# A two-pass mixer with sixty gathered expert rows inside it, and two alternating stages for the gate matrices

## The chip, the cores and the metric

The kernel is one launch on one core of one Trainium2 chip. The metric is device time in microseconds (us). The time given for the kernel before is the median of 3 runs, 4351.54 us (4319.0 to 4370.52).

## What is computed

One layer of a hybrid model for 1024 prompt tokens and 8 sample tokens: attention of two kinds (latent attention, and three groups of dilated windows), a gated mixer that adds their outputs to the residual, and then an expert layer. Width is 1024. What matters here is the end of the layer:

```python
y = gate_a * (o_mla @ lw['w_branch_mla']) + gate_b * (o_dil @ lw['w_branch_dil'])
x = x + gt1 * (y @ lw['w_out'])
h2 = modulate(x, lw['norm_ffn_g'], sh2, sc2)
x = x + gt2 * peer(h2, lw['w_pq'], lw['sub_keys'], lw['expert_u'], lw['expert_v'])
...
def peer(h, w_pq, sub_keys, expert_u, expert_v):
        q = (hx @ w_pq).reshape(PEER_BLOCK, PEER_HEADS, 2, PK_HALF)
        s = jnp.einsum('nhpc,hpkc->nhpk', q, sub_keys).astype(jnp.float32)
        top_s, top_i = lax.top_k(s, PEER_TOPK)
...
        best_s, best = lax.top_k(cand.reshape(PEER_BLOCK, PEER_HEADS, PEER_TOPK * PEER_TOPK), PEER_TOPK)
...
        a = jax.nn.gelu(jnp.einsum('nd,nhkd->nhk', hx, expert_u[eidx]), approximate=False) * g
        return jnp.einsum('nhk,nhkd->nd', a, expert_v[eidx])
```

The gates are sigmoids of the hidden state times `w_gate`. There are 16384 experts, and each token uses 16 experts in each of 8 heads: 128 rows of `expert_u` and 128 of `expert_v` (kept side by side in `uv`, 8 KB for a pair).

## The kernel before, in words

Tokens are cut into eight tiles of 128 and a ninth of 8. Everything of this part is kept with features on the partitions and tokens along the free side.

**The mixer, `stage_mix` (L1546).** It goes over 24 units, 8 blocks of 128 output features times 3 chunks of 344 tokens. For a unit TensorE does 8 fp32 branch products (L1630; the trace counts an fp32 matmul as two) and 48 products of split weights: a weight or activation w is kept as a rounded high part and a low part, and `product3` (L177 to L179) multiplies high by high, low by high, high by low. ScalarE makes the high part of a weight (L1579), VectorE the low part (L184); ScalarE takes the sigmoids (L1664), VectorE mixes (L1695, L1698). After all units the mixed y is split in the same way and goes through `w_out` in 24 units of 24 products. Squares, their sums over the features (L1617), roots, and the scaled h2 end the stage. All engines meet at its end.

**The expert layer, `stage_ffn` (L1832).** It has four stretches.

1. The early router: for 16 half heads (hp) the query of tiles 0 and 1 (L2356), the scores (L2346), the best 16 of 128 on VectorE (`top16`, L1954 to L1961). Then 48 transposes (L2402) turn h2 of the six sparse tiles into rows, and VectorE picks the experts of tile 0: the five pieces of `Picks`.
2. Batches. Sparse tiles (0 to 4 and the 8 sample tokens) get their experts by gathers. A batch is two gathered rows for each of 128 tokens, that is two indirect DMAs on GpSimd's queue (L2035) of 128 x 8 KB, 2.1 MB together. VectorE takes two dot products with the token's row (L2137); ScalarE applies gelu and the gate (L2219, L2222) and, for the first two tiles, writes a diagonal matrix (L2231), with which TensorE adds the rows up (L2463). Batches 3, 6, ... 45 (`ON_VEC`) are added up by VectorE instead (L2087). The ring `rows` holds five batches, and a gather waits until the sum of five batches before has read its place. Batches 0 to 47 carry the late router, one half head in three batches, for the other seven tiles (L2411, L2346, `top16`). From batch 51 on the pieces of the three dense tiles (5, 6, 7) and, from 61 on, their gate matrices are made: 96 quads (L2163, L2170, L2301, L2303, L2435), two in a batch, copied by ScalarE into `stage` (L2313) and written to DRAM (`gates_dram`) 16 quads at a time; the next block waits for that write.
3. Batch 128 on: the dense loop. Every one of 128 turns multiplies the three dense tiles with 128 experts (L2474, L2488), with 0.5 MB of `uT` and of `v` loaded for it; beside it run the remaining 196 batches, three in two turns, summed on VectorE (L2103).
4. The outputs are turned, added and stored.

The order on each engine is what this code says; the numbers of batches, pieces and quads come from the tables at L1845 to L1862.

## Time and profile before

| what | value |
| --- | --- |
| median of 3 runs | 4351.54 us |
| profiled execution | 4370.86 us, its span 4369.1 us |
| mean granted TensorE clock | 0.913 |
| PE busy | 3802.1 us (87%) |
| DVE (VectorE) busy | 2723.7 us (62%) |
| ACT (ScalarE) busy | 1199.4 us (27%) |
| moved by DMA | 1016.29 MB, 233 GB/s over the span |

PE is TensorE's matmuls, PEld its weight loads, POOL GpSimd, SP the queue that issues most loads. A busy share over the whole span says little here, since the stretches have different limits; they have to be read one by one.

### The profile page before, as it was taken

How to read it: one execution, taken by the hardware profiler on the slowest of the kernel's cores; microseconds unless marked ns; L12 is line 12 of the kernel's file. 1: busy time of each engine (PE TensorE's matmuls, PEld its weight loads, DVE VectorE, ACT ScalarE, POOL GpSimd, SP SyncE). 2: the span in 40 equal slices, each digit the busy share in tenths (PEclk: the TensorE clock that was granted, in tenths of full speed). 3: DMA queues.
4: the chain of work that ended last, by engine and by line, in shares of the span. 5: the costliest groups of instructions: out<-in, count | busy, mean ns of one | idle time of the engine just before them, and what ended most of it. 6: DMA issues, size and time to landing. Idle time of an engine off the chain costs nothing.

```text
span 4369.1 us, 43255 instructions
## 1 busy us (share of the span) xinstructions
PE 3802.1 (87%) x14474; PEld 2490.1 (57%) x14474; DVE 2723.7 (62%) x6374; ACT 1199.4 (27%) x3244; POOL 859.8 (20%) x718
## 2 busy tenths in 40 slices
PE   8798899999981899967997677799999999899896
PEld 7575377888970788953453444344454444445443
DVE  2764562533534111258999987767779676967876
ACT  2564432322332111122222567421111111111111
POOL 0000000001000000003333223333333333344332
PEclk8898998995985899988999888899999999999997
DMA  4001102203116111237888879999999999999997
GB/s 158 7 1 42 29 37 80 81 20 119 51 40 208 55 41 36 100 108 282 323 327 318 314 302 376 399 417 409 410 399 378 414 412 387 384 409 412 387 354 279
DMA packets 255851, 1016.29 MB, mean 233 GB/s; under 512 B 28650, under 2 KB 103810, under 8 KB 170642
## 3 DMA queue, kind: packets, MB, share of 16 engines
q0 software_dynamic: 101520, 723.10, 41.9%
q1 hardware_dynamic: 131218, 280.65, 17.4%
q10 hardware_dynamic: 22896, 9.80, 0.8%
q8 instruction: 117, 1.92, 0.2%
q14 instruction: 100, 0.82, 0.1%
HBM read 964.22 MB, written 49.25 MB: 232 GB/s over the span
## 4 chain that ended last, share of the span: by engine, by line
PE 27%; DVE 15%; DMA 11%; issue 2%; ACT 2%; SPq 0%; POOL 0%; ACTq 0%; DVEq 0%
PE banks L2488 9%; PE banks L2474 9%; DMA ff_room<-in_v 7%; PE banks L2463 4%; DVE ff_rows L2137 4%; PE banks L2411 2%; DVE ff_acc L2103 2%; DMA gates_dram<-ff_room 2%; PE banks L2356 1%; DMA ff_rows<-in_uv,pk_expert 1%; DVE pk_eq L1793 1%; DVE pk_axes L1798 1%; DVE mx_x L2163 1%; PE banks L2435 1%; DVE pk_besti L1772 1%
## 5 line engine op out<-in xcount | busy, mean ns | idle before, releaser
L2035 POOL DMA_INDIRECT ff_rows<-in_uv,pk_expert x640 | 803.0, 1255 | 1519.2 <-DVE ff_acc L2103 831.8
L2137 DVE CUSTOM_DVE_ANT_0 ff_rows<-ff_rows,ff_h_row 128x1024 f32<-128x1024 f32 x648 | 766.6, 1220 | 45.3 <-DMA ff_rows<-in_uv,pk_expert 43.4
L2488 PE MATMUL banks<-ff_room,mx_x 128*128 128x512 f32 x1536 | 702.3, 608 | 57.9 <-DVE mx_x L2178 31.2
L2474 PE MATMUL banks<-mx_x,ff_room 128*128 128x384 f32 x2048 | 685.7, 488 | 12.2 <-ACT mx_x L2321 12.2
L2463 PE MATMUL banks<-ff_rows,o_mla_tops 128*128 128x512 f32 x904 | 446.5, 643 | 144.5 <-ACT o_mla_tops L2231 140.8
L2474 PEld LDWEIGHTS banks<-mx_x,ff_room 128*128 128x128 f32 x2048 | 390.3, 191 | 313.0 <-issue 77.3
L2488 PEld LDWEIGHTS banks<-ff_room,mx_x 128*128 128x128 f32 x1536 | 297.3, 195 | 418.9 <-issue 357.8
L2103 DVE SCALAR_TENSOR_TENSOR ff_acc<-ff_rows,ff_a,ff_acc 128x1024 f32<-128x1024 f32 x388 | 498.6, 1285 | 7.2
L2463 PEld LDWEIGHTS banks<-ff_rows,o_mla_tops 128*128 128x128 f32 x904 | 179.1, 206 | 361.8 <-issue 198.5
L177 PE MATMUL banks<-d_w_high,h_high 128*128 128x512 f32 (+1 forms) x648 | 274.3, 423 | 21.9 <-DVE d_w_low L184 21.0
L2219 ACT ACTIVATE ff_gelu<-ff_dots 128x2 f32<-128x2 f32 x324 | 65.7, 203 | 824.9 <-DVE ff_dots L2137 824.7
L178 PE MATMUL banks<-d_w_low,h_high 128*128 128x512 f32 (+1 forms) x648 | 264.4, 408 | 0.0
L179 PE MATMUL banks<-d_w_high,h_low 128*128 128x512 f32 (+1 forms) x648 | 263.8, 407 | 0.0
L2178 DVE TENSOR_TENSOR mx_x<-mx_x 128x384 f32<-128x384 f32 x128 | 71.3, 557 | 293.8 <-DMA mx_x<-gates_dram 162.1
L2321 ACT ACTIVATE mx_x<-banks 128x384 f32<-128x384 f32 x128 | 62.6, 489 | 626.0 <-PE banks L2474 626.0
L754 DVE TENSOR_TENSOR banks<-banks,masks 128x128 f32<-128x128 f32 (+1 forms) x160 | 53.6, 335 | 255.0 <-PE banks L665 240.3
L177 PEld LDWEIGHTS banks<-d_w_high,h_high 128*128 128x128 f32 (+1 forms) x648 | 166.5, 257 | 46.6 <-DVE d_w_low L184 10.4
L179 PEld LDWEIGHTS banks<-d_w_high,h_low 128*128 128x128 f32 (+1 forms) x648 | 166.7, 257 | 20.4
L178 PEld LDWEIGHTS banks<-d_w_low,h_high 128*128 128x128 f32 (+1 forms) x648 | 167.7, 259 | 18.2
L2411 PE MATMUL banks<-mx_x,ff_room 128*128 128x388 f32 x512 | 173.3, 491 | 0.0
L1695 DVE TENSOR_TENSOR mx_t<-mx_sig,banks 128x344 f32<-128x344 f32 x48 | 22.4, 509 | 236.6 <-ACT mx_sig L1664 236.6
L2222 ACT ACTIVATE ff_a<-ff_gelu,pk_gate 128x1 f32<-128x1 f32 x640 | 153.5, 287 | 11.0
(391 smaller groups left out, 5660.3 us busy)
## 6 DMA issues: line engine op xcount, KB each, us to landing
ff_room<-in_uT SPq DMA_DIRECT2D x128, 512.0 KB, 14.4
ff_room<-in_v SPq DMA_DIRECT2D x128, 512.0 KB, 20.6
gates_dram<-ff_room SPq DMA_DIRECT2D x6, 4096.0 KB, 16.8
mx_x<-gates_dram SPq DMA_DIRECT2D x128, 192.0 KB, 17.2
d_w<-in_w_dil POOLq DMA_DIRECT2D x9, 2048.0 KB, 8.3
d_w<-in_w_ada POOLq DMA_DIRECT2D x32, 512.0 KB, 4.7
ff_room<-in_w_pq SPq DMA_DIRECT2D x32, 512.0 KB, 4.5
ff_rows<-in_uv,pk_expert POOLq DMA_INDIRECT x640, 10.8
```

Source lines behind the costliest of these rows:

```text
L177: pe.matmul(out, w[0], x[0], start=start, stop=False)
L178: pe.matmul(out, w[0], x[1], start=False, stop=False)
L179: return pe.matmul(out, w[1], x[0], start=False, stop=stop)
L2035: pool.indirect_dma_start(out=rows[r][:, :], out_offset=None, in_=IN["uv"][:, :], in_offset=bass.IndirectOffsetOnAxis(ap=at, axis=0))\
L2103: ins = dve.scalar_tensor_tensor(out=y[:], in0=v, scalar=weight, in1=y[:], op0=ALU.mult, op1=ALU.add)
L2137: ins = dve.tensor_tensor_reduce(rows[r][:, 0:D], rows[r][:, 0:D], h_row[i % 2][:], 1.0, 0.0, ALU.mult, ALU.add, dots[:, B % RB, j:j + 1])
L2178: dve.tensor_tensor(blocks(ad[e % 2]), blocks(ge[e % 2]), g2[e // 2 % 2][:, :, :, e % 2], ALU.mult)\
L2222: ins = act.activation(a[:, B % RB, j:j + 1], act_of[:, B % RB, j:j + 1], ACT.Copy, scale=gt[:, b * G + j:b * G + j + 1])
L2411: ins = pe.matmul(Q[:, i, 0:CL], w[n % 2][:, k, :], c.h2[:, k, NE + i * CL:NE + (i + 1) * CL], start=(k == 0), stop=(k == KD - 1))
L2463: ins = pe.matmul(A[:, half], diag[:, n % DB, j], rows[r][:, D + half * 512:D + (half + 1) * 512], **ends)
L2474: ins = pe.matmul(SD[:, 0:ND], u[e % 4][:, k, :], hd[:, k, :], start=(k == 0), stop=(k == KD - 1))
L2488: ins = pe.matmul(Y[j][:, half], ad[e % 2][:, j * P:(j + 1) * P], v[e % 4][:, half_rows[half]], start=(e == 0), stop=(e == NK - 1))
```

## The change

`stage_mix` is written anew. Pass 0 takes tiles 0 and 1 (256 tokens, `NE`) through the gates, through `w_out`, to h2. Pass 1 takes the other 776 tokens in two chunks of 388. A unit is now one side (one of the two branches) of one block of features and one chunk: 16 in pass 0, 32 in pass 1. Each weight is loaded and split in both passes. After the second unit of pass 1 the whole early router stands on TensorE, ScalarE and VectorE (here with the names `mx_rows` for its space and `px_` for its picks), then 8 transposes for the rows of tile 0, and on VectorE the pieces of tile 0. From unit z = 5 of pass 1 on, 30 batches (60 gathered rows for each token of tile 0) run in the mixer: 24 beside gate units, 6 beside output units. Their dots and sums are both VectorE's. Their ring holds two batches.

```diff
 PAGE, NPAGE, PAST = 128, 8, 1024
 PH, NK, TOPK = 8, 128, 16
...
     nc, IN = c.nc, c.IN
-    KO = GW // P
+    KO, HP, G, NE = GW // P, 2 * PH, 2, EARLY * P
+    CB = (TOK - NE) // 2
+    PASSES = [[(0, NE)], [(NE, NE + CB), (NE + CB, TOK)]]
+    SUBS = [(p, m, side, i) for p in range(2) for m in range(KD) for side in range(2) for i in range(len(PASSES[p]))]
+    OUTS2 = [(p, m, i) for p in range(2) for m in range(KD) for i in range(len(PASSES[p]))]
+    S1, O1, W1 = 2 * KD, KD, 3 * KD
+    NB, RB = MIX_BATCHES, 2
+    ROUTER_AT = 1
+    BATCH_AT = [z for z in range(5, 31) if z not in (16, 28)] + list(range(33, 48, 2))
+    batch_at = {z: b for b, z in enumerate(BATCH_AT[0:NB])}
...
+        ringR, ring = same_place(c, ctx, [P, RB * G, 2 * D], [("mx_rows_high", F32R), ("mx_rows", F32)])
...
+                    if m == 2:
+                        sp.dma_start(keys, IN["keysT"]).then_inc(s["keys_in"], 16)
+                    if m == 3:
+                        queries(0)
...
+                for n in range(S1, S1 + 4):
+                    weight(n)
+                sp.wait_ge(s["mm"], S1)
+                residual(0)
+                for n in range(S1 + 4, W1):
+                    weight(n)
+                branch(KD)
+                branch(KD + 1)
+                weight(W1)
+                weight(W1 + 1)
+                keep(0)
+                weight(W1 + 2)
+                for n in range(2, HP):
+                    queries(n)
+                weight(W1 + 3)
+                for m in range(2, KD):
+                    branch(KD + m)
...
+            @block.gpsimd
+            def _(pool):
+                pool.wait_ge(s["half_tile"], 1)
+                for b in range(NB):
+                    for j in range(G):
+                        r = b % RB * G + j
+                        if b >= RB:
+                            pool.wait_ge(s["rsum"], (b - RB) * G + j + 1)
+                        at = c.expert0[:, b * G + j:b * G + j + 1]
+                        pool.indirect_dma_start(out=ring[:, r, :], out_offset=None, in_=IN["uv"][:, :],
+                                                in_offset=bass.IndirectOffsetOnAxis(ap=at, axis=0))\
+                            .then_inc(rows_in[r], 16)
...
+                def gated(u):
+                    p, m, side, i = SUBS[u]
+                    c0, c1 = PASSES[p][i]
+                    n, b = p * W1 + 2 * m + side, p * KD + m
+                    gate, out = c.ps[2 * (u % 3)][:, 0:c1 - c0], c.ps[2 * (u % 3) + 1][:, 0:c1 - c0]
...
+                    if S1 <= u < S1 + 3:
+                        pe.wait_ge(s["out"], (O1 - 2, O1, O1)[u - S1])
...
+                    if u >= 3:
+                        pe.wait_ge(s["y"], u - 2)
+                    src = c.o_dilT if side else c.o_mlaT
+                    for k in range(KO):
+                        pe.matmul(out, wb[b % 2][:, side * KO + k, :], src[:, k, c0:c1], start=(k == 0), stop=(k == KO - 1))
+                    pe.wait_ge(s["w_lo"], n + 1)
+                    for k in range(KD):
+                        ins = product3(pe, gate, w_parts(n, k), [t[:, k, c0:c1] for t in h_parts], k == 0, k == KD - 1)
+                    ins.then_inc(s["mm"], 1)
...
+                for u in range(S1):
+                    gated(u)
+                pe.wait_ge(s["y"], S1)
+                for v in range(O1):
+                    projected(v)
+                squares_sum(0, KD - 1)
+                for u in range(S1, len(SUBS)):
+                    gated(u)
+                    if u == S1 + ROUTER_AT:
+                        pe.wait_ge(s["keys_in"], 16)
+                        pe.wait_ge(s["h2"], KD)
+                        queries(0)
+                        for hp in range(HP):
+                            if hp + 1 < HP:
+                                queries(hp + 1)
+                            scores(hp)
...
+                def weights(b):
+                    act.wait_ge(s["dot"], b + 1)
+                    act.activation(act_of[:, b % RB], dots[:, b % RB], ACT.Gelu).then_inc(s["gelu"], 1)
+                    act.wait_ge(s["gelu"], b + 1)
+                    for j in range(G):
+                        ins = act.activation(a[:, b % RB, j:j + 1], act_of[:, b % RB, j:j + 1], ACT.Copy,
+                                             scale=c.gate0[:, b * G + j:b * G + j + 1])
+                    ins.then_inc(s["a"], 1)
...
+                for z in range(len(SUBS) - S1):
+                    sigmoid(S1 + z)
+                    for n in made_after(S1 + z):
+                        w_high(act, n)
+                    if z == ROUTER_AT:
+                        copied_queries(0)
...
+                    if z == 3:
+                        pk.exps(act, 0)
+                    if z in batch_at:
+                        weights(batch_at[z])
...
+                def dot(b):
...
+                    if b >= RB:
+                        dve.wait_ge(s["a"], b - RB + 1)
+                    for j in range(G):
+                        r = b % RB * G + j
+                        dve.wait_ge(rows_in[r], 16 * (b // RB + 1))
+                        u = ring[:, r, 0:D].rearrange("p (k n) -> p k n", n=NE)
+                        ins = dve.tensor_tensor_reduce(u, u, h_row, 1.0, 0.0, ALU.mult, ALU.add, dots[:, b % RB, j:j + 1])
+                    ins.then_inc(s["dot"], 1)
...
+                def sums(b):
+                    dve.wait_ge(s["a"], b + 1)
...
+                        else:
+                            dve.wait_ge(s["rsum"], b * G + j)
+                            ins = dve.scalar_tensor_tensor(out=acc, in0=v, scalar=weight, in1=acc, op0=ALU.mult, op1=ALU.add)
+                        ins.then_inc(s["rsum"], 1)
+
+                def sums_due(z):
+                    if z in batch_at and batch_at[z]:
+                        sums(batch_at[z] - 1)
+
+                def dots_due(z):
+                    if z in batch_at:
+                        dot(batch_at[z])
...
+                for z in range(len(SUBS) - S1):
+                    sums_due(z)
+                    mixed(S1 + z)
+                    for n in made_after(S1 + z):
+                        w_low(dve, n)
+                    if z == ROUTER_AT:
+                        for hp in range(HP):
+                            dve.wait_ge(s["sc_copy"], hp + 1)
+                            for part in range(4):
+                                top16(part, hp)
+                                dve.wait_ge(s["top"], hp * 4 + part + 1)
+                        pk.prepare(dve)
+                        picks(0)
+                        picks(1)
+                    if 2 <= z <= 4:
+                        picks(z)
+                    dots_due(z)
+                y_low(1)
+                w_low(dve, W1 + 2 * KD + 1)
+                for m in range(KD):
+                    for n in made_beside(1, m):
+                        if n > W1 + 2 * KD + 1:
+                            w_low(dve, n)
+                    for i in range(2):
+                        sums_due(32 + 2 * m + i)
+                        added(O1 + 2 * m + i)
+                        dots_due(32 + 2 * m + i)
+                sums(NB - 1)
+                normed(1)
```

In `stage_ffn` tile 0 keeps batches 30 to 63 only, so that tile 1 begins at batch 34 (by the new numbering, which is used for the changed kernel from here on) and the dense loop at 98. Three quads are made in a batch, from batch 58 to 89. The gate blocks go to two stages in turn; the second lies in four of the ten gather rows, and from batch 56 to 95 the ring therefore holds three batches (`FEW`). VectorE's own sums (`ON_VEC`) stand at batches 3 to 30. The rows of tiles 2 to 4 and of the samples are stored by SP, not by GpSimd.

```diff
-    batches = [(i, b) for i in range(NS) for b in range(TAILB if i == TAIL else PER)]
-    first = [batches.index((i, 0)) for i in range(NS)] + [len(batches)]
-    ORDER = [0, 1] + DENSE + [2, 3, 4, NT - 1]
+    batches = [(i, b) for i in range(NS) for b in range(0 if i else MIX_BATCHES, TAILB if i == TAIL else PER)]
+    first = [batches.index((i, 0 if i else MIX_BATCHES)) for i in range(NS)] + [len(batches)]
+    ORDER = [1] + DENSE + [2, 3, 4, NT - 1]
...
-    PICK0, HOT0, HOTS = HP * LATE_PER + 3, HP * LATE_PER + 13, 2
+    PICK0, HOT0, HOTS = HP * LATE_PER + 3, HP * LATE_PER + 10, 3
...
-    TURN0 = 112
+    TURN0 = 86
     OUT_AT = 44
-    PIECES = {4 + 8 * k: (1, k) for k in range(5)}
-    PIECES |= {PICK0 + 10 * j + 2 * k: (t, k) for j, t in enumerate(DENSE) for k in range(5)}
-    PIECES |= {PICK0 + 59 + 3 * k: (2, k) for k in range(5)}
+    PIECES = {2 + 6 * k: (1, k) for k in range(5)}
+    PIECES |= {PICK0 + at + step * k: (t, k) for t, at, step in zip(DENSE, (0, 6, 16), (1, 2, 2)) for k in range(5)}
+    PIECES |= {PICK0 + 29 + 3 * k: (2, k) for k in range(5)}
     PIECES |= {first[i + 1] - 12 + 2 * k: (SPARSE[i + 1], k) for i in range(ON_PE, TAIL - 1) for k in range(5)}
...
-    ON_VEC = list(range(LATE_PER, HP * LATE_PER, LATE_PER))
+    ROWS_ORDER = [0] + list(range(2, NS)) + [1]
+    ON_VEC = list(range(LATE_PER, first[1] - 1, LATE_PER))
...
+    FEW, FEW_AT, MANY_AT = 3, HOT0 - 2, HOT0 + QUADS // HOTS + 6
+    place = [B % FEW if FEW_AT <= B < MANY_AT else (B - (0 if B < FEW_AT else first[TAIL])) % RB for B in range(len(batches))]
...
-        stage = part(0, NK * GBLK).rearrange("p (a n) -> p a n", n=GBLK)
+        second = ring[:, FEW * G:FEW * G + 4].rearrange("p r f -> p (r f)")
+        stage = [t.rearrange("p (a n) -> p a n", n=GBLK) for t in (part(0, NK * GBLK), second)]
...
                     sp.wait_ge(s["hot_copy"], (k + 1) * BQ)
-                    sp.dma_start(gates[k].rearrange("p a n -> p (a n)"), stage.rearrange("p a n -> p (a n)"))\
-                      .then_inc(s["g_out"], 16)
-                sp.wait_ge(s["g_out"], 16 * (QUADS // BQ))
+                    sp.dma_start(gates[k].rearrange("p a n -> p (a n)"), stage[k % 2].rearrange("p a n -> p (a n)"))\
+                      .then_inc(g_out[k % 2], 16)
+                for k in range(2):
+                    sp.wait_ge(g_out[k], 16 * (QUADS // BQ // 2))
...
-                    if B - RB in ON_VEC:
-                        pool.wait_ge(s["early"], by_vec(B - RB) * G)
-                    elif RB <= B < BP + RB:
-                        pool.wait_ge(s["psum"], by_pe(B - RB))
-                    elif B >= RB:
-                        pool.wait_ge(s["sum"], (B - RB - BP + 1) * G)
-                    if B == PER // 2:
-                        pool.wait_ge(pk.done, 1)
+                    if B == MANY_AT:
+                        pool.wait_ge(g_out[1], 16 * (QUADS // BQ // 2))
+                    if last[B] in ON_VEC:
+                        pool.wait_ge(s["early"], by_vec(last[B]) * G)
+                    elif last[B] is not None and last[B] < BP:
+                        pool.wait_ge(s["psum"], by_pe(last[B]))
+                    elif last[B] is not None:
+                        pool.wait_ge(s["sum"], (last[B] - BP + 1) * G)
...
+                                act.wait_ge(s["top"], 4 * HP)
+                            elif q == BQ:
+                                act.wait_ge(s["psum"], by_pe(FEW_AT - 1))
                             else:
-                                act.wait_ge(s["g_out"], 16 * (q // BQ))
+                                act.wait_ge(g_out[q // BQ % 2], 16 * (q // BQ // 2))
```

Three places show what the engines now have in a row. The first is TensorE where the mixer ends and the expert layer begins. Before, with the router's queries (L2356) ahead of the transposes (L2402):

```order
4517 L1617 MATMUL banks<-o_mla_tops,ones 128x344 x6
4518 L1589 UNCONDITIONAL_BRANCH
4519 L2336 UNCONDITIONAL_BRANCH
4520 L2356 MATMUL banks<-mx_x,ff_room 128x256 x16
4521 L2346 MATMUL banks<-ff_room 128x128 x2
...
4547 L2346 MATMUL banks<-ff_room 128x128 x2
4548 L2356 MATMUL banks<-mx_x,ff_room 128x256 x8
4549 L2346 MATMUL banks<-ff_room 128x128 x4
4550 L2402 MATMUL banks<-ident,mx_x 128x128 x24
4551 L2402 MATMUL banks<-ident,mx_x 8x128 x8
4552 L2402 MATMUL banks<-ident,mx_x 128x128 x16
4553 L2411 MATMUL banks<-mx_x,ff_room 128x388 x6
4554 L2463 MATMUL banks<-ff_rows,o_mla_tops 128x512 x4
```

and in the changed kernel (L2707 is a transpose, L2719 a late query, L2771 a sum of gathered rows):

```order
4554 L182 MATMUL banks<-mx_y_high,mx_w_low 128x388
4555 L1729 MATMUL banks<-o_mla_tops,ones 128x388 x4
4556 L1641 UNCONDITIONAL_BRANCH
4557 L2658 UNCONDITIONAL_BRANCH
4558 L2707 MATMUL banks<-ident,mx_x 128x128 x32
4559 L2707 MATMUL banks<-ident,mx_x 8x128 x8
4560 L2707 MATMUL banks<-ident,mx_x 128x128 x8
4561 L2719 MATMUL banks<-mx_x,ff_room 128x388 x6
4562 L2771 MATMUL banks<-ff_rows,o_mla_tops 128x512 x4
```

The queries and scores of 16 half heads have left this place; the 48 transposes stand first.

The second is VectorE in pass 1 of the mixer, where before only weights were split (L184) and units mixed (L1695, L1698):

```order
1587 L1695 TENSOR_TENSOR mx_t<-mx_sig,banks 128x344 x2
1588 L1698 TENSOR_TENSOR mx_y<-mx_t 128x344
1589 L184 TENSOR_TENSOR mx_w_low<-mx_w,mx_w_high 128x2048
1590 L1695 TENSOR_TENSOR mx_t<-mx_sig,banks 128x344 x2
1591 L1698 TENSOR_TENSOR mx_y<-mx_t 128x344
1592 L1695 TENSOR_TENSOR mx_t<-mx_sig,banks 128x344 x2
1593 L1698 TENSOR_TENSOR mx_y<-mx_t 128x344
```

In the changed kernel, from the unit z = 7 on (L1996 a dot, L2007 a sum of a gathered row into tile 0's total, which lies in `region`, L1927 to L1930 the mixing, L187 the low part of a weight):

```order
1823 L2007 SCALAR_TENSOR_TENSOR region<-mx_rows,mx_a,region 128x1024 x2
1824 L1929 TENSOR_TENSOR mx_sig<-mx_sig,banks 128x388
1825 L1930 TENSOR_TENSOR mx_y<-mx_y,mx_sig 128x388
1826 L1996 ISA mx_rows,mx_dots<-mx_rows,o_mla_tops 128x1024
1827 L1996 ISA mx_dots 128x1
1828 L1996 ISA mx_rows,mx_dots<-mx_rows,o_mla_tops 128x1024
1829 L1996 ISA mx_dots 128x1
1830 L2007 SCALAR_TENSOR_TENSOR region<-mx_rows,mx_a,region 128x1024 x2
1831 L1927 TENSOR_TENSOR mx_y<-mx_sig,banks 128x388
1832 L187 TENSOR_TENSOR mx_w_low<-mx_w,mx_w_high 128x1024
1833 L1996 ISA mx_rows,mx_dots<-mx_rows,o_mla_tops 128x1024
1834 L1996 ISA mx_dots 128x1
```

Between two units there now stand two dots and two sums.

The third is ScalarE beside it, again of the changed kernel (L1823 the sigmoid, L1622 the high part of a weight, L1864 gelu, L1867 the gate):

```order
1038 L1823 ACTIVATE mx_sig<-banks 128x388
1039 L1864 ACT_TABLE_LOAD
1040 L1864 ACTIVATE mx_gelu<-mx_dots 128x2
1041 L1867 ACTIVATE mx_a<-mx_gelu,region 128x1 x2
1042 L1823 ACT_TABLE_LOAD
1043 L1823 ACTIVATE mx_sig<-banks 128x388
1044 L1622 ACTIVATE mx_w_high<-mx_w 128x1024
1045 L1864 ACT_TABLE_LOAD
1046 L1864 ACTIVATE mx_gelu<-mx_dots 128x2
1047 L1867 ACTIVATE mx_a<-mx_gelu,region 128x1 x2
1048 L1823 ACT_TABLE_LOAD
```

A table load stands before each sigmoid and before each gelu; before, the mixer's gate units had one in all.

## Rows read from the trace of the kernel before

**Rows 1.** Windows by stage; columns: length, then busy us (instructions) of each engine, clock, DMA
```profile
core 0: us, PE busy (x) PEld busy (x) DVE busy (x) ACT busy (x) POOL busy (x), PEclk, DMA share, GB/s
1448.60:1877.80 429.20, 403.69 (x2160) 356.44 (x2160) 103.39 (x149) 70.93 (x93) 0.00 (x0) 0.97 0.15 54
1877.80:1976.80 99.00, 79.94 (x367) 65.31 (x368) 59.31 (x300) 18.70 (x43) 2.15 (x4) 0.86 0.37 123
1976.80:2334.40 357.60, 314.73 (x980) 169.46 (x979) 326.93 (x1206) 86.58 (x287) 111.98 (x104) 0.96 0.84 319
2334.40:2892.70 558.30, 417.87 (x1451) 230.10 (x1450) 468.98 (x1328) 297.22 (x768) 180.49 (x162) 0.87 0.89 351
2893.00:4321.00 1428.00, 1354.09 (x3608) 690.08 (x3607) 1084.75 (x1577) 197.33 (x714) 524.30 (x393) 0.98 1.00 397
```
**Rows 2.** Timeline of PE: split products of 344 columns in the mixer, of 512 earlier
```profile
1602.04 0.32 PE L179 MATMUL banks<-h_high,mx_w_low 128*128 128x344 f32 x1
...
1609.10 0.32 PE L179 MATMUL banks<-h_high,mx_w_low 128*128 128x344 f32 x1
...
699.88 0.39 PE L177 MATMUL banks<-d_w_high,h_high 128*128 128x512 f32 x1
...
702.66 0.39 PE L177 MATMUL banks<-d_w_high,h_high 128*128 128x512 f32 x1
```
**Rows 3.** Chain of waits, early router: start, us, what (one half head of sixteen)
```profile
1893.74 3.71 PE banks L2356 x16
1898.06 3.71 PE banks L2356 x16
```
**Rows 4.** Chain of waits, late router: one half head, three batches
```profile
2218.88 7.82 PE banks L2411 x24
2226.70 3.43 PE banks L2463 x8
...
2235.69 3.63 PE banks L2463 x8
2239.32 7.82 PE banks L2411 x24
```
**Rows 5.** Timeline of DVE: picks of tile 0, and dots and sums in the dense loop
```profile
1961.02 1.23 DVE L1765 TENSOR_TENSOR pk_cand<-o_mla_tops 128x1024 f32<-128x1024 f32 x1
1977.36 0.23 DVE L1815 SCALAR_TENSOR_TENSOR pk_expert<-pk_axes 128x64 uint32<-128x64 f32 x1
1995.71 0.22 DVE L1815 SCALAR_TENSOR_TENSOR pk_expert<-pk_axes 128x64 uint32<-128x64 f32 x1
...
2951.24 1.22 DVE L2137 CUSTOM_DVE_ANT_0 ff_rows<-ff_rows,ff_h_row 128x1024 f32<-128x1024 f32 x1
2952.39 2.64 DVE L2103 SCALAR_TENSOR_TENSOR ff_acc<-ff_rows,ff_a,ff_acc 128x1024 f32<-128x1024 f32 x2
2960.08 0.56 DVE L2178 TENSOR_TENSOR mx_x<-mx_x 128x384 f32<-128x384 f32 x1 [2.75 <-DMA mx_x<-gates_dram]
```
**Rows 6.** Timeline of ACT: a table load, gelu and gate of the first batch
```profile
1994.81 1.28 ACT L2219 ACT_TABLE_LOAD   x1
1998.38 0.20 ACT L2219 ACTIVATE ff_gelu<-ff_dots 128x2 f32<-128x2 f32 x1 [2.29 <-DVE ff_dots L2137]
1998.62 0.48 ACT L2222 ACTIVATE ff_a<-ff_gelu,pk_gate 128x1 f32<-128x1 f32 x2
```
**Rows 7.** Windows from batch 51 to the dense loop; then VectorE's waits there, longest first
```profile
2352.20:2892.70 540.50, 403.18 (x1409) 223.29 (x1408) 453.57 (x1261) 290.06 (x743) 173.39 (x155) 0.87 0.89 353
...
DVE ff_rows L2137 <- DMA ff_rows<-in_uv,pk_expert: 43.4, 24, 5.3
DVE mx_x L2163 <- PE banks L2435: 35.0, 6, 9.8
```
**Rows 8.** DMA issues in the mixer and in the late router: size, median us to landing
```profile
mx_w<-in_w_gate SPq DMA_DIRECT2D x12, 512.0 KB, 5.5
...
ff_rows<-in_uv,pk_expert POOLq DMA_INDIRECT x88, 8.1
```

635 lines of the change are left out of this document (386 added, 249 removed).

## The prediction

> **What bounds the kernel now.** I read the windows by stage first [rows 1], since the shares over the whole span mix stretches with different limits. The mixer takes 429.2 us, and TensorE is busy in 403.7 of them: it is the bound, VectorE is busy for a quarter, and the DMA engines for 0.15. The early router and the turning of rows take 99.0 us, again nearly all TensorE's. Then come 357.6 us of batches under the late router. There the chain of waits steps by 20.44 us for one half head and three batches (2218.88 to 2239.32), and all but 1 us of a step is on TensorE [rows 4]. The next 558.3 us belong to VectorE, busy for 469.0. The dense loop has a DMA share of 1.00 at 397 GB/s: TensorE is busy for 1354 of 1428 us beside it, but the bytes set the pace [rows 1].
>
> So the kernel has a mixer in which the DMA engines idle and a dense loop in which they are full. The change takes 30 of the 64 batches of tile 0 out of the stretch before the dense loop and puts them beside the mixer. The dense loop keeps its 196 batches, its 128 turns and its bytes: I take its 1428 us, and everything before the mixer, as unchanged.
>
> **The mixer.** TensorE's work first. A split product of 344 columns comes every 0.157 us (45 of them in 7.06 us), one of 512 every 0.232 (12 in 2.78) [rows 2]. The trace has none of 256 or 388 columns; on the line through the two they are 0.118 and 0.177. Bounds for the 256 ones: 0.116 if they went with the columns alone (0.232 x 256 / 512), and 0.157 if something other than the columns sets the pace below 344, which no row excludes; the 192 + 384 products of pass 0 would then cost 22 us more. I take the line, since 344 and 512 lie close to one rate. A half of an fp32 product costs 7.82 / 24 = 0.326 us at 388 columns [rows 4], so 0.289 at 344, and 3.71 / 16 = 0.232 at 256 [rows 3].
>
> - Before: 24 units of 48 x 0.157 + 16 x 0.289 = 12.2, 292 us; 24 output units of 24 x 0.157 and 48 halves for the squares, 104. Together 396; the other 33 us are the start, the splitting of y between the two parts, and the end (roots, reciprocals, h2).
> - After: pass 0 has 16 units of 24 x 0.118 + 8 x 0.232 = 4.7, 75 us, and 8 output units of 3.3, 26. Pass 1 has 32 units of 24 x 0.177 + 8 x 0.326 = 6.85, 219 us, and outputs of 16 x 4.24 + 32 x 0.326 = 78. Together 398: cutting the tokens in two costs TensorE 2 us. The ends, now with two changes from gates to outputs but fewer columns in the last, are 34. Weights are loaded and split twice. A weight lands in 5.5 us [rows 8] and pass 0 has four places for them, so this hides behind units of 4.7 us; if it did not, each of 16 weights would cost up to 1 us.
> - The root, the reciprocal and h2 of pass 0 (about 10 us) hide behind the first two units of pass 1, 13.7 us. Then the router: 16 x 4.32 us [rows 3], and with its filling and 8 transposes 73 us. It stays pure TensorE time, as before.
> - After it VectorE is late. It ends the last `top16` about 3.7 us after TensorE's scores, and the first half of the picks is 16.5 us (1961.02 to 1977.6 [rows 5]); then it mixes and splits the weight of the third pair, at 22. TensorE needs that weight after its transposes, two units and four branch products, at 18.3. The second half of the picks is 18.4 us (1977.4 to 1995.9) and delays the next weight likewise, by 7. I charge 11 us.
> - From then on a unit with a batch costs VectorE two dots of 1.15 and the read (2.38), the wait for gelu and gate (0.72 on ScalarE [rows 6], 0.85 with signals), two sums 2.6, mixing 0.56 or twice that (0.87 in the mean), half a low part 0.6 (it has the 1024 columns of a dot), and 0.15 for signals: 7.45 us [rows 5]. TensorE needs 6.85. Over the 27 units from z = 5 on this is 24 x 7.45 + 3 x 1.5 = 183 against 185, with three banks' worth of slack between the engines. Balanced, then; I charge 10 us for what two balanced engines lose to each other here and beside the outputs. The added wait is the one for the gate, at the head of the sums: behind it on VectorE stand the mixing and the low part, for which TensorE waits.
> - The gathers: from the end of the first sum of a batch to the first dot two batches on VectorE has 10.2 us of other work; a landing takes 8.1 [rows 8]. Hidden, by a small margin.
> - ScalarE now has two table loads of 1.28 us [rows 6] a unit. With gelu and gate 0.7, sigmoid 0.5, half a high part 0.5, that is 4.3 of 7.45, and the load for gelu has no dependency and runs ahead of its wait, as the one at 1994.81 did. Cost: nothing.
>
> The Trainium skill ("ScalarE: Activation LUTs", What ACT_TABLE_LOAD costs) speaks against this: a switch costs 2.66 us, since a drain of 1.38 us goes with the load. By that ScalarE would need 7.1 us a unit, and the mixing would wait 0.3 us a unit for its sigmoid, 7 us in all. The row shows 1.28 and no drain, but the engine was idle behind it, so the trace doesn't decide.
>
> Sum: 398 + 73 + 11 + 10 + 34 = 526 us for 429.2, so **+97**.
>
> **The expert layer up to the dense loop.** Before, batch 51 begins 474.4 us after the stage's start (2352.2 less 1877.8). After: the 48 transposes are 22 us (99.0 less 69 for the half heads, less some 8 for the first weights and the filling [rows 1, 3]), and 3 go to a store in their middle. These stores now stand in SP's queue ahead of the third query weight, which is wanted 40 us later. The gathers start with the stage, so TensorE doesn't wait for the first batch as it did. 11 half heads of 20.44 and, because `ON_VEC` ends with batch 30, 5 that carry a third batch on TensorE, each 3.43 more [rows 4]: 344 us. Then 18 us of `top16` and dots as before (2334.4 to 2352.2). 387: **-87**, of which 70 is the router that moved into the mixer.
>
> From batch 51 on VectorE was busy for 453.6 of 540.5 us [rows 7]. Quads and pieces stay as many; 30 batches go, 60 dots of 1.15 = 69 us, leaving 385. Of its 87 us of idle time 35.0 were waits for quads behind a gate block that was being written, 43.4 waits for gathered rows [rows 7]. The second stage removes the 35, since a block now has five batches until its place is wanted again. The waits for rows I leave at 40: fewer batches, but a shorter ring. 385 + 40 + 8 = 433: **-107**.
>
> Total: 97 - 87 - 107 = -97 us on the profiled 4371, 4274. That run was slow against the median 4351.54; the same 2.2% of it gives **4255 us**.
>
> **The rivals.**
>
> 1. The rings are too short. From batch 56 to 95 a gather waits for the sum three batches before: dots 2.3, gelu, gate and diagonal 1.4, sum 3.43, two issues 2.5, landing 8.1 make 17.7 us, and ScalarE can be late with the quads by 5. Three batches of 9.2 (433 / 47) are 27.6, but batches without a piece are near 7, and a gate block of 4 MB in front can double a landing. For: VectorE waited 24 times for rows even with five batches. Price: 3 us in 20 batches, 60 us; and in the mixer a landing of 14 instead of 8.1 costs (14 - 10.2) / 2 in 30 batches, 57. One of them gives 4313, both 4371.
> 2. The other way, the rings keep up, the waits for rows fall with the load (40 to 10), and TensorE and VectorE lose nothing to each other: 4274 - 40, scaled 4215 or less.
> 3. Slower than before: the ring of two in the mixer decides alone. It cancels the gain where a landing takes 10.2 + 2 x 97 / 30 = 16.7 us, and passes 1% at 19.6 (44 us more, 4395). The mixer also reloads 17 MB, but its DMA share is 0.15 and the gathers add about 0.7; a median of 8.1 at a share of 0.84 [rows 1, 8] speaks against it.
> 4. The table switches cost the page's price: 4262.
>
> **Chances.** The sum as made (4215 to 4300) 0.55, too-short rings 0.20, better 0.15, slower 0.05, table switches 0.05. A measurement of this kernel can tell about 1% from no change. Faster by over 1% (below 4308) takes the first, the third, the last and a quarter of the rings: 0.80; within 1% 0.15; slower 0.05. The range, 4190 to 4335, leaves out the worse half of the rings and the slower case.
>
> **What would show it.** In the changed profile: the mixer ends near 1975 us; split products of 256 columns come every 0.118 us; gate units of pass 1 with a batch come every 7 to 7.6 us, TensorE stands still twice after the router, 4 and 7 us; the first dense product is near 2795, with the dense loop still at 1428 us; ScalarE's waits for the gate write are gone; VectorE's waits for rows before the dense loop are near 40 us, and few in the mixer. Wrong would be: units of 9 us or more, waits for rows over 80 us, or a dense loop whose length moved by more than 20 us, since its bytes did not.

## The result, and the profile of the changed kernel

| what | before | after |
| --- | --- | --- |
| median | 4363.84 us (4319.0 to 4371.42, 11 runs) | 4293.51 us (4259.48 to 4309.49, 11 runs) |
| ratio to before | 1 | 0.985, 95% interval 0.9821 to 0.9879 |
| span of the profiled execution | 4369.1 us | 4302.4 us |

The changed kernel is faster by 1.5%, where the prediction said 2.2% (4255 of 4351.54; range 4190 to 4335). Both profiles have the same mean clock, 0.913, so their stages can be set side by side: 66.7 us less in the span, for 97 forecast. Part of the distance between 4255 and 4293.51 is not the kernel's: the forecast was scaled to 4351.54, the median of 3 runs of before, and over 11 runs that median is 4363.84.

The windows by stage of the changed kernel answer to [rows 1]: the mixer with the early router in it; the transposes; the rest of the late router; batch 51 to the first dense product; the dense loop with the outputs (length, busy us of PE, PEld, DVE, ACT, POOL, clock, DMA share, GB/s).

```profile
core 0: us, PE busy (x) PEld busy (x) DVE busy (x) ACT busy (x) POOL busy (x), PEclk, DMA share, GB/s
1448.60:1973.30 524.70, 475.40 (x2482) 415.99 (x2480) 354.26 (x727) 203.73 (x327) 100.85 (x60) 0.96 0.60 216
1973.30:2003.70 30.40, 12.71 (x47) 7.81 (x48) 8.68 (x14) 6.55 (x11) 9.37 (x10) 0.50 0.97 384
2003.70:2373.60 369.90, 346.50 (x1068) 183.95 (x1066) 304.18 (x1201) 96.38 (x321) 109.30 (x101) 0.99 0.81 304
2373.60:2825.10 451.50, 316.81 (x1166) 190.55 (x1165) 382.24 (x1141) 249.17 (x592) 101.91 (x94) 0.83 0.73 281
2825.10:4302.40 1477.30, 1365.12 (x3657) 697.63 (x3655) 1114.10 (x1636) 203.63 (x729) 528.21 (x394) 0.97 0.98 388
```

| stretch, us | before | forecast | after |
| --- | --- | --- | --- |
| mixer, up to the turning of rows (before: up to the stage's end) | 429.2 | 526 | 524.7 |
| expert layer's start to batch 51 | 474.4 | 387 | 400.3 |
| batch 51 to the first dense product | 540.5 | 433 | 451.5 |
| from there to the end | 1475.5 | same | 1477.3 |

The mixer's row is cut at 1448.60 us, where the mixer of before begins. In the changed kernel the first branch product stands at 1445.5, so its own mixer takes 527.9 us and the code ahead of it, which is not changed, 3.1 us less; it spreads by far more than that (see the experiments). From the first branch product to the end it is 2920.5 us before and 2856.9 after, 63.6 less.

So the mixer came out within 2 us of its forecast by either cut, and the loop did not move. The missing 30 us lie in the two stretches between.

**The mixer.** TensorE's timeline in pass 0 (start, us, line, shapes) shows a split product of 256 columns, of which [rows 2] had none:

```profile
1499.96 0.28 PE L181 MATMUL banks<-h_low,mx_rows_high 128*128 128x256 f32 x1
...
1500.89 0.28 PE L180 MATMUL banks<-h_high,mx_rows_high 128*128 128x256 f32 x1
```

Eight products in 0.93 us: one every 0.116 (0.1175 over five others), for 0.118 forecast. In pass 1 a unit with 388 columns begins here and the next one there:

```profile
1745.94 0.64 PE L180 MATMUL banks<-h_high,mx_w_high 128*128 128x388 f32 x1
...
1750.32 0.34 PE L182 MATMUL banks<-h_high,mx_w_low 128*128 128x388 f32 x1
1750.50 2.77 PE L1747 MATMUL banks<-o_dilT,mx_w_branch 128*128 128x388 f32 x8
1752.80 0.64 PE L180 MATMUL banks<-h_high,mx_w_high 128*128 128x388 f32 x1
```

A unit takes 6.86 us, TensorE's own 6.85 of the forecast, and not VectorE's 7.45. Two windows, one behind the router and one over the units with batches:

```profile
1645.00:1690.00 45.00, 35.39 (x147) 28.36 (x148) 41.13 (x117) 9.00 (x12) 4.35 (x4) 0.89 0.35 129
1690.00:1867.00 177.00, 176.72 (x820) 148.89 (x819) 146.59 (x191) 99.19 (x153) 78.58 (x46) 0.99 0.86 312
```

In the first TensorE stands still for 9.6 us (2.87 and 6.75, for 4 and 7 forecast) and waits for the low part of a weight, since VectorE picks experts. In the second it is busy for 176.72 of 177 us beside 2.1 MB of gathered rows a unit, at a DMA share of 0.86. The ring of two, in which the slower case lay, is never waited for at length: of VectorE's waits in the whole mixer this line is all of that kind.

```profile
DVE mx_rows L1996 <- DMA mx_rows<-in_uv,region: 5.9, 7, 2.3
```

**Between the mixer and the dense loop.** The chain of waits at the stage's start (start, us, what) shows the turning of rows (L2707) with two long stores in it.

```profile
1984.17 11.30 DMA h_rows<-ff_h_row
...
1997.80 4.56 DMA h_rows<-ff_h_row
...
2003.04 1.11 PE banks L2707 x4
```

ScalarE can overwrite its place for turned rows (L2585) only when SP's store of them has landed. The window from 1973.30 to 2003.70 above has a DMA share of 0.97: the gathers of five batches, 10.5 MB, start at the same time (experiment 7 holds four of them back).

Behind the transposes ScalarE's copy of a query (L2520) marks each half head: the first at 2023.47 us, the sixteenth at 2356.35. Of the fifteen steps between them six are the forecast's 20.44 to 0.01 us and the last four its 23.87, with three sums in each:

```profile
2311.45 3.63 PE banks L2771 x8
2315.08 3.91 PE banks L2719 x12
...
2329.77 2.62 PE banks L2719 x8
...
2335.33 3.63 PE banks L2771 x8
```

But one step is 26.50 us, from 2105.41 to 2131.91. In it the chain lies on VectorE, with picks of tile 1 (L2096 to L2110), dots, sums and the late `top16` in a row:

```profile
2107.00 1.24 DVE pk_cand L2096
...
2114.50 1.61 DVE pk_besti L2110 x4
...
2122.29 1.21 DVE region L2411
```

The step of 21.60 has picks in its chain too (L2119 to L2135). The one of 25.59 lies on TensorE: a third sum, and 1.72 us of four products (L2766) that take over VectorE's sums of tile 0 where its batches end. With these two the fifteen take 332.9 us where the forecast's are 324 (ten of 20.44 and five of 23.87).

VectorE's waits from batch 51 to the dense loop answer to [rows 7] (us, times, longest):

```profile
DVE ff_rows L2460 <- DMA ff_rows<-in_uv,pk_expert: 60.1, 16, 15.5
DVE ff_rows L2460 <- DMA ff_rows<-in_uv,region: 2.5, 2, 1.4
DVE mx_x L2486 <- PE banks L2743: 1.2, 1, 1.2
```

The 35.0 us behind the gate blocks are 1.2, as said. Its busy time is 382.24 us, for 385. But the waits for rows are 62.6, for 40. The timeline shows where they lie: 12 us in one place, at batches 58 and 59,

```profile
2431.07 1.23 DVE L2460 CUSTOM_DVE_ANT_0 ff_rows<-ff_rows,ff_h_row 128x1024 f32<-128x1024 f32 x1 [9.68 <-DMA ff_rows<-in_uv,pk_expert]
...
2434.68 1.23 DVE L2460 CUSTOM_DVE_ANT_0 ff_rows<-ff_rows,ff_h_row 128x1024 f32<-128x1024 f32 x1 [2.38 <-DMA ff_rows<-in_uv,pk_expert]
```

9 us at two gate blocks (2532 and 2637 us), and 42 us in the last 57 before the dense loop. That last part has a bound of its own, in the changed kernel and before the change:

```profile
2768.50:2825.10 56.60, 32.02 (x60) 12.74 (x59) 14.82 (x25) 9.87 (x36) 19.71 (x18) 0.85 0.95 381
```

```profile
2836.00:2893.60 57.60, 44.30 (x89) 18.46 (x90) 37.40 (x65) 18.02 (x58) 22.43 (x20) 0.85 1.02 419
```

The first line is the changed kernel's, the second that of before. VectorE, which bounds the stretch as a whole, has 15 us of work in 57 (before: 37 in 58), at a DMA share of 0.95 (1.02).

### The profile page after: what moved, and what is told of

Read it like the earlier page. It is cut to its first block, busy times and chain, and to the rows that moved or that the text cites. A ratio compares the mean times of both kernels' runs of the same rounds, so it can differ in the third digit from the quotient of the medians.

```text
span 4302.4 us, 43216 instructions
## 1 busy us (share of the span) xinstructions
PE 3735.0 (87%) x14282; PEld 2465.9 (57%) x14282; DVE 2813.1 (65%) x6473; ACT 1282.9 (30%) x3304; POOL 888.3 (21%) x714
## 4 chain that ended last, share of the span: by engine, by line
PE 23%; DVE 15%; DMA 13%; issue 2%; ACT 1%; SPq 0%; POOL 0%; DVEq 0%; ACTq 0%; POOLq 0%
DMA ff_room<-in_v 9%; PE banks L2796 8%; PE banks L2782 8%; DVE ff_rows L2460 4%; PE banks L2771 3%; PE banks L2719 3%; DVE mx_x L2486 2%; DMA ff_rows<-in_uv,pk_expert 2%; DMA mx_x<-gates_dram 1%; DVE region L2426 1%; DVE pk_eq L2124 1%; DVE o_mla_tops L2129 1%; DVE mx_x L2493 1%; DVE ff_acc L2426 1%; DVE pk_besti L2110 1%
## 5 line engine op out<-in xcount | busy, mean ns | idle before, releaser
L2460 DVE CUSTOM_DVE_ANT_0 ff_rows<-ff_rows,ff_h_row 128x1024 f32<-128x1024 f32 x588 | 696.5, 1221 | 86.9 <-DMA ff_rows<-in_uv,pk_expert 61.0
L2371 POOL DMA_INDIRECT ff_rows<-in_uv,region x324 | 418.6, 1292 | 808.6 <-DVE region L2426 540.9
L2371 POOL DMA_INDIRECT ff_rows<-in_uv,pk_expert x256 | 314.2, 1227 | 754.0 <-PE banks L2771 414.6
L2771 PE MATMUL banks<-ff_rows,o_mla_tops 128*128 128x512 f32 x704 | 356.7, 655 | 95.1 <-ACT o_mla_tops L2554 95.1
L2426 DVE SCALAR_TENSOR_TENSOR region<-ff_rows,ff_a,region 128x1024 f32<-128x1024 f32 x254 | 326.5, 1286 | 4.7
L2542 ACT ACTIVATE ff_gelu<-ff_dots 128x2 f32<-128x2 f32 x294 | 59.5, 203 | 846.0 <-DVE ff_dots L2460 845.8
L2771 PEld LDWEIGHTS banks<-ff_rows,o_mla_tops 128*128 128x128 f32 x704 | 142.2, 210 | 270.7 <-issue 152.6
L757 DVE TENSOR_TENSOR banks<-banks,region 128x128 f32<-128x128 f32 (+1 forms) x160 | 53.6, 335 | 256.8 <-PE banks L668 240.0
L1719 POOL DMA_INDIRECT mx_rows<-in_uv,region x60 | 100.8, 1681 | 508.7 <-DVE region L2146 342.9
L2719 PE MATMUL banks<-mx_x,ff_room 128*128 128x388 f32 x512 | 175.1, 493 | 0.0
## 6 DMA issues: line engine op xcount, KB each, us to landing
gates_dram<-ff_rows SPq DMA_DIRECT2D x3, 4096.0 KB, 15.9
```

Source lines behind the costliest of these rows:

```text
L1719: pool.indirect_dma_start(out=ring[:, r, :], out_offset=None, in_=IN["uv"][:, :], in_offset=bass.IndirectOffsetOnAxis(ap=at, axis=0))\
L2371: pool.indirect_dma_start(out=rows[r][:, :], out_offset=None, in_=IN["uv"][:, :], in_offset=bass.IndirectOffsetOnAxis(ap=at, axis=0))\
L2426: ins = dve.scalar_tensor_tensor(out=y[:], in0=v, scalar=weight, in1=y[:], op0=ALU.mult, op1=ALU.add)
L2460: ins = dve.tensor_tensor_reduce(rows[r][:, 0:D], rows[r][:, 0:D], h_row[i % 2][:], 1.0, 0.0, ALU.mult, ALU.add, dots[:, place[B], j:j + 1])
L2719: ins = pe.matmul(Q[:, i, 0:CL], w[n % 2][:, k, :], c.h2[:, k, NE + i * CL:NE + (i + 1) * CL], start=(k == 0), stop=(k == KD - 1))
L2771: ins = pe.matmul(A[:, half], diag[:, n % DB, j], rows[r][:, D + half * 512:D + (half + 1) * 512], **ends)
```

## Experiments

All times are set beside the changed kernel, 4293.51 us. Every profile is split like the table above, each at its own instructions. What lies ahead of the mixer is the same code in all of them, and takes from 1403.5 us (granted clock 0.88 there) to 1452.8 us (0.85). That is 49 us, over 1% of a kernel's time, without any edit; so differences are read from stretches and not from the whole. The last column leaves that part out. It is one profile of each kernel.

| kernel | median, us | ratio to before | first branch product to the end, us |
| --- | --- | --- | --- |
| changed | 4293.51 | 0.985 | 2856.9 |
| 1 one stage | 4308.0 | 0.9877 | 2866.3 |
| 2 blocks in four parts | 4287.08 | 0.9851 | 2854.8 |
| 2 blocks not written | 4283.54 | 0.9821 | 2831.1 |
| 3 exponentials later | 4299.6 | 0.985 | 2858.2 |
| 4 ends of the ring | 4288.66 | 0.9815 | 2849.8 |
| 5 twelve batches | 4361.73 | 0.9991 | 2909.3 |
| 6 sums on VectorE | 4276.21 | 0.9796 | 2833.6 |
| 7 gathers held | 4297.11 | 0.9851 | 2852.4 |
| 8 no table switches | 4292.02 | 0.9863 | 2848.3 |

Of the intervals given below only that of experiment 5 is clear of the changed kernel's (0.9821 to 0.9879). For all the others a difference in the kernel's whole time is not shown.

### 1. One stage, a ring of five

```diff
-    FEW, FEW_AT, MANY_AT = 3, HOT0 - 2, HOT0 + QUADS // HOTS + 6
+    FEW, FEW_AT, MANY_AT = 5, HOT0 - 2, HOT0 + QUADS // HOTS + 6
...
-        stage = [t.rearrange("p (a n) -> p a n", n=GBLK) for t in (part(0, NK * GBLK), second)]
+        stage = [t.rearrange("p (a n) -> p a n", n=GBLK) for t in (part(0, NK * GBLK),)] * 2
...
-                                act.wait_ge(g_out[q // BQ % 2], 16 * (q // BQ // 2))
+                                act.wait_ge(g_out[(q // BQ - 1) % 2], 16 * ((q // BQ + 1) // 2))
```

> Undoes the second stage alone: one stage for the gate blocks, the ring keeps five batches, three quads in a batch as in the changed kernel. Theory A (a 4 MB gate write in front of the gathers makes them land late, and three batches are too few to cover it): VectorE's waits for rows from batch 51 to the dense loop fall from 62 us to 10 to 25, but waits for quads behind the write return, 50 to 70 us, so the stretch is 450 to 470 us for 451, the kernel 0 to 20 us slower than the changed one. Theory B (the second stage is worth the 35 us of the sum): 30 us slower or more, stretch over 480.

Measured 4308.0 us, ratio to before 0.9877 (0.983 to 0.9923). VectorE's waits from batch 51 on:

```profile
DVE mx_x L2483 <- PE banks L2738: 42.6, 11, 8.6
DVE ff_rows L2457 <- DMA ff_rows<-in_uv,pk_expert: 22.1, 6, 11.9
DVE ff_rows L2457 <- DMA ff_rows<-in_uv,region: 3.0, 2, 1.6
```

The waits for quads are back, 42.6 us, but those for rows fall from 62.6 to 25.1, and the stretch is 455.7 us for 451.5. So the second stage removes what it was to remove and gives nearly all of it back through the four gather rows that it takes: it is worth 4 us in this stretch. The waits for rows that are left all lie behind 2798 us, in the last 35 us before the dense loop.

### 2. Gate blocks written in four parts, and not at all

```diff
-                    sp.dma_start(gates[k].rearrange("p a n -> p (a n)"), stage[k % 2].rearrange("p a n -> p (a n)"))\
-                      .then_inc(g_out[k % 2], 16)
+                    for j in range(4):
+                        if j:
+                            sp.wait_ge(s["dot"], HOT0 + (16 * k + 15) // HOTS + 2 + j)
+                        rows_of = slice(j * NK // 4, (j + 1) * NK // 4)
+                        sp.dma_start(gates[k][:, rows_of], stage[k % 2][:, rows_of]).then_inc(g_out[k % 2], 16)
```

> The changed kernel with each gate block written in four DMAs of 1 MB instead of one of 4 MB, the second to fourth waiting for the dots of the next three batches. Theory A (a gather stands behind 4 MB of gate block): waits for rows in that stretch fall from 62 us to 20 to 35, stretch 451 to about 420, kernel 25 to 35 us faster than the changed one. Rival (the ring of three is too short by itself, with any traffic): waits stay over 50 us, no change within 10 us.

Measured 4287.08 us, ratio 0.9851 (0.9798 to 0.9905): the stretch is 448.0 us, the waits for rows 58.9, those at the two blocks 5.3 us for 8.9. That a gather stands behind 4 MB in one piece is not what makes most of the 62.6 us. The other kernel writes a 128th of each block and takes the gates from elsewhere, so it leaves the gate matrices out of the result:

```diff
-                    sp.dma_start(gates[k].rearrange("p a n -> p (a n)"), stage[k % 2].rearrange("p a n -> p (a n)"))\
-                      .then_inc(g_out[k % 2], 16)
+                    sp.dma_start(gates[k][:, 0], stage[k % 2][:, 0]).then_inc(g_out[k % 2], 16)
...
-                            src = gates[half * GB:(half + 1) * GB, :, e:e + 2].rearrange("b p a n -> p b a n")
+                            src = IN["xT"][:, half * GB:(half + 1) * GB, 0:2 * GBLK].rearrange("p b (a n) -> p b a n", n=GBLK)
```

> The changed kernel with the gate blocks not written (32 KB of each remain) and the dense loop loading other values of the same size and row length in their place: it leaves the gate matrices out of the result. Ring, quads and copies stay as they are. Theory A (gathers land late behind the block writes): waits for rows from batch 51 on fall from 62 us to under 15, the stretch from 451 to about 400 us. Rival (the short ring by itself): waits stay over 45 us, stretch over 435.

Measured 4283.54 us, ratio 0.9821 (0.9768 to 0.9874). Its waits:

```profile
DVE ff_rows L2459 <- DMA ff_rows<-in_uv,pk_expert: 45.9, 12, 11.6
DVE ff_rows L2459 <- DMA ff_rows<-in_uv,region: 2.5, 2, 1.4
```

Without any write 48 of 62.6 us are still there; the stretch is 438.3 us, 13 less. The 12 us at batches 58 and 59 are unchanged (9.45 and 2.42 us), those at the two blocks are gone, and the last ones fall from 42 to 37. That is the rival on record (waits over 45 us, a stretch over 435), though the stretch is 13 us shorter.

### 3. Exponentials a batch later

In the changed kernel the chain went through ScalarE at these blocks: it stood for a piece's exponentials (L2141), then made three quads, and only then took gelu of the next batch (L2542), so that the sum that frees the ring came late.

```profile
2504.45 0.31 ACT pk_best L2141
...
2508.42 2.73 ACT ff_room L2635 x3
2511.16 1.28 ACT L2542
...
2519.17 15.93 DMA ff_rows<-in_uv,pk_expert
```

```diff
-                    if B in PIECES and PIECES[B][1] == 3:
-                        pk.exps(act, PIECES[B][0])
+                    if B - 1 in PIECES and PIECES[B - 1][1] == 3:
+                        pk.exps(act, PIECES[B - 1][0])
```

> The changed kernel, but ScalarE takes the exponentials of a piece one batch later, behind the next batch's gelu, gate and diagonal instead of ahead of them. Theory (the ring of three is short because ScalarE stands waiting for a piece's differences, makes three quads, and only then the gate of the next batch, so that TensorE's sum and with it the gather come late): VectorE's waits for rows between batch 51 and the dense loop fall from 62.6 to 25 to 35 us, that stretch from 451.5 to 420 to 430, the kernel is 20 to 30 us shorter than the changed one. Rival (the ring and the landings alone are too slow for a batch of 9 us, whatever ScalarE does): waits for rows stay at 55 or more, the time within 6 us.

Measured 4299.6 us, ratio 0.985 (0.9819 to 0.9882): the rival. The stretch is 450.7 us and the waits for rows are 58.9. Of the 3.7 us less, 3.2 are at batches 58 and 59 (8.9 for 12.1), and only 0.3 at the two blocks (8.5 for 8.9). The chain at the same block now has no ScalarE work of that kind, but a longer landing:

```profile
2506.73 3.71 PE banks L2771 x8
2510.71 1.09 POOL ff_rows L2371
2512.10 17.45 DMA ff_rows<-in_uv,pk_expert
2529.57 1.23 DVE ff_rows L2460
```

The gather starts 1.0 us behind the block, whose write was issued at 2511.13, where in the changed kernel it started 2.5 us behind it (2519.17 and 2516.72). It takes 17.45 us to land instead of 15.93. So in both kernels it lands 18.4 us behind the block's issue (at 2529.55 and 2535.10). In these 18.4 us 7.1 MB are moved, at a DMA share of 0.97 (here 7.2 MB in 18.5 us, share 0.96): the block's 4.2 MB and 2.9 MB of rows. The bytes decide when it lands, and ScalarE's place in the chain, which looked like the cause, was worth 0.3 us of waits at the blocks. VectorE now waits 3.1 us for the exponentials themselves.

### 4. The two ends of the ring of three

With the places of the ring written out, batch 57 takes place 0 of the ring of three, the place of batch 55, two before it; 58 is queued behind it on GpSimd. At the other end batches 96 and 97 take the places of 94 and 95, and wait for the last block's write as well.

```diff
-    FEW, FEW_AT, MANY_AT = 3, HOT0 - 2, HOT0 + QUADS // HOTS + 6
-    place = [B % FEW if FEW_AT <= B < MANY_AT else (B - (0 if B < FEW_AT else first[TAIL])) % RB for B in range(len(batches))]
+    FEW, FEW_AT, MANY_AT = 3, HOT0, first[2] + 3
+    place = [(B - FEW_AT) % FEW if FEW_AT <= B < MANY_AT else (B - (0 if B < FEW_AT else first[TAIL])) % RB for B in range(len(batches))]
```

> The changed kernel with the two changes of the ring placed otherwise: the ring of three begins at batch 58 instead of 56, its places counted so that every batch takes the place of the one three before (in the changed kernel batch 57 takes the place of 55, two before, and 58 stands queued behind it), and it ends at batch 101 instead of 96 (there batches 96 and 97 take the places of 94 and 95, two before, and wait for the write of the last gate block as well). Theory (the waits for rows come not from the ring of three as such, but from its two ends: 12 us at batches 58 and 59, and a gather that stands 21 us before batch 96): VectorE's waits for rows between batch 51 and the dense loop fall from 62.6 to 30 to 40 us, the first 12 us vanish, that stretch from 451.5 to 425 to 435, the kernel is 15 to 25 us shorter than the changed one. Rival (the end is limited by bytes: the last gate block of 4 MB, seven batches and the first loads of the dense loop): only the first 12 us go, waits near 50, stretch near 440. Second rival (what is saved is waited for again in the dense loop's first turns): the stretch shrinks and the rest grows by as much.

Measured 4288.66 us, ratio 0.9815 (0.9786 to 0.9844), 5 us less than the changed kernel where the theory said 15 to 25. The stretch is 437.8 us, 13.7 less, with waits of

```profile
DVE ff_rows L2460 <- DMA ff_rows<-in_uv,pk_expert: 44.8, 15, 15.5
DVE ff_rows L2460 <- DMA ff_rows<-in_uv,region: 4.8, 2, 2.7
```

The 12 us are gone (0.6 left). The ones before the dense loop are not (39 us for 42): the first rival, and its forecast of 440. The second rival has a part in it too: within the dense loop VectorE waits 9.2 us for rows, where the changed kernel had 0.9, and the rest takes 1480.1 us for 1477.3. The windows of this kernel, up to the last block and from there to the first dense product, say why:

```profile
2378.50:2765.00 386.50, 281.50 (x1111) 178.51 (x1110) 367.40 (x1118) 241.15 (x564) 83.07 (x77) 0.84 0.71 274
2765.00:2816.30 51.30, 30.68 (x56) 12.00 (x56) 14.25 (x23) 7.85 (x29) 14.43 (x14) 0.80 1.01 408
```

In the last 51 us the DMA share is 1.01, at 408 GB/s, and VectorE has 14 us of work. The quads and pieces are done, and what is left is bytes: a gate block, the rows of the last batches and the first loads of the dense loop, 20.9 MB (51.3 x 408). A gathered batch of 2.1 MB costs 5.1 us at that rate, where its two dots cost 2.3.

The bytes are not the whole of it. In both kernels GpSimd starts no gather for 12.73 us just ahead of this window (up to 2764.62 here, to 2770.23 in the changed kernel). It waits for TensorE's sums, which stand behind a piece, the last quads and their copies on VectorE and ScalarE. From 2762 to 2769 us the changed kernel has a DMA share of 0.37. Then the block, three batches and the first loads start together, and the longest wait of all, 15.5 us, follows. No run takes this pause away, so how much of the 39 us it makes is not shown.

### 5. Twelve batches in the mixer instead of thirty

```diff
-EARLY, MIX_BATCHES = 2, 30
+EARLY, MIX_BATCHES = 2, 12
```

> The changed kernel with 12 batches in the mixer instead of 30 (18 more in the expert layer, five more half heads with a batch summed by VectorE). My account (TensorE bounds the mixer and the batches hide behind it): mixer 525 to 510 to 517 us; the expert layer up to the dense loop 18 batches of about 8 to 9 us longer, less 17 for the half heads, +130; kernel 115 to 130 us slower than the changed one. Rival (the gathers cost the mixer what they save later): mixer shorter by 60 us or more, kernel slower by under 70.

Measured 4361.73 us, ratio 0.9991 (0.9964 to 1.0017): with twelve batches nothing is left of the gain. Its windows, the mixer, the stretch from batch 51, and the end of that stretch:

```profile
1438.00:1957.20 519.20, 475.84 (x2489) 418.71 (x2490) 268.76 (x620) 160.35 (x248) 38.57 (x24) 0.97 0.43 147
2339.70:2879.40 539.70, 383.81 (x1315) 216.55 (x1314) 426.57 (x1214) 274.96 (x683) 144.06 (x131) 0.87 0.77 304
2800.00:2879.40 79.40, 60.25 (x128) 23.66 (x129) 39.03 (x64) 20.64 (x75) 37.04 (x31) 0.98 1.01 421
```

The mixer is 9 us shorter than the changed kernel's (527.9, from its first branch product), 0.5 us a batch: they are hidden there. (The same mixer code takes 524.8 to 532.2 us in eleven profiles, so it is 0.3 to 0.7.) The stretch from batch 51 is 88 us longer, 44 of it VectorE's work and 44 waits for rows (106.2 for 62.6 us), and the late router ahead of it 16 shorter; the dense loop with the outputs is 9 shorter too. From the mixer's start to the end 52 us, by medians 68: a batch that is moved is worth 2.9 to 3.8 us.

The forecast of 115 to 130 us was too high by about two. It priced a batch in this stretch at 8 to 9 us, the mean of batches that have quads and pieces beside them. Those stay; a batch more costs 4.9 us (88 / 18). That is near the price of its bytes: in the last 79 us the DMA share is 1.01 at 421 GB/s, which makes 5.0 us for 2.1 MB, and VectorE works for 39. And since twelve batches in the mixer only bring the time of before, the rest of the rewriting, two passes and a router in the mixer, brings nothing by itself. By the slope of 2.9 to 3.8 us a batch it would cost 35 to 45 us, an estimate: no kernel without any batch in the mixer was run.

### 6. Every third batch of tile 1 on VectorE

```diff
-    ON_VEC = list(range(LATE_PER, first[1] - 1, LATE_PER))
+    ON_VEC = list(range(LATE_PER, first[1] - 1, LATE_PER)) + list(range(first[1] + 2, HP * LATE_PER, LATE_PER))
+    VEC1 = len([n for n in ON_VEC if n < first[1]])
...
-                        if B + 1 == first[1]:
-                            pe.wait_ge(s["early"], len(ON_VEC) * G)
+                        if B + 1 in (first[1], first[2]):
+                            pe.wait_ge(s["early"], (VEC1, len(ON_VEC))[i] * G)
```

> The changed kernel with batches 36, 39, 42 and 45, of tile 1, summed on VectorE too, so that half heads 12 to 15 have two batches on TensorE instead of three. My step (TensorE bounds these half heads, 3.43 us each for the third batch): four steps of 23.87 us become 20.44, the late router 352 to about 338 us, the kernel 10 to 14 us faster. Rival (VectorE is the bound there as well): no change, under 4 us.

Measured 4276.21 us, ratio 0.9796 (0.9732 to 0.986). The late router behind the transposes takes 355.4 us for 369.9, and the chain has the step of 20.44 again (2298.15 to 2318.59):

```profile
2298.15 7.82 PE banks L2726 x24
...
2318.59 7.82 PE banks L2726 x24
```

That is 14.5 us for four steps of 3.43 (13.7), as forecast. It was then put together with three of the other edits.

> Both changes together, four more batches of tile 1 summed on VectorE and the gate blocks written in four pieces. Theory A and the bound by TensorE in the late router: 35 to 45 us faster than the changed kernel, since they act in different stretches; 4250 us for a profiled 4302. If neither holds, no change.

> Two edits together: the exponentials one batch later, and every third batch of tile 1 (36 to 45) summed on VectorE. If the two gains are in different stretches they add up: the late router 14 us shorter (355 for 369.5 us), the stretch from batch 51 to the dense loop 20 to 30 us shorter, together 35 to 40 us less than the changed kernel, a ratio to the kernel before near 0.975. If the exponentials turn out worth nothing, this is the time with the sums alone, 4276 us.

> The same, and every third batch of tile 1 (36 to 45) summed on VectorE, which alone was worth 14 us in the late router. Both gains lie in different stretches: the late router 355 us, the next stretch as in the run with the places alone, the ratio to the kernel before near 0.975 by the theory, 0.978 by the rival.

Measured: with the gate blocks in four parts 4278.0 us (0.9804, 0.9762 to 0.9846), with the later exponentials 4281.39 (0.9803, 0.9772 to 0.9835), with the ring's ends 4277.06 (0.98, 0.9776 to 0.9824). All four kernels with the sums on VectorE lie within 5 us of each other, 12 to 17 us below the changed kernel; from the first branch product to the end their profiles take 2830.2 to 2837.7 us, 19 to 27 less than its. The sums' 14 us are there each time, though no interval alone is clear of the changed kernel's. The further gains that were forecast for the blocks in parts and for the ring's ends did not come: beyond the sums the gains don't add up. With the ring's ends the stretch from batch 51 is 437.4 us, 13.1 less than with the sums alone, but the dense loop and the outputs are 7.1 longer and the mixer, whose code is the same, 4.9: 2832.7 us from the mixer's start to the end, for 2833.6. The waits for rows in the dense loop rise here too, from 0.9 to 8.3 us. By medians the ring's ends are worth 5 us alone and none here: how much of the 13 us reaches the end of the kernel stays open.

### 7. Gathers held until the rows are stored

```diff
+                    if B == 1:
+                        for k in range(2):
+                            pool.wait_ge(h_out[k], 32)
```

> The changed kernel, but GpSimd starts the gathers of its second batch in the expert layer only when the stores of h2's rows have landed. Theory (the stores land late, 11.3 and 4.6 us of waiting, because five batches of gathers fill the DMA engines just as the stage starts): the transposes take 22 to 25 us in place of 30.3; the kernel is between 0 and 7 us shorter, since the gathers of batches 1 to 4 start some 20 us later and may be waited for in turn. Rival (the stores are late by their own place in SP's queue or by their size): the transposes stay at 29 to 31 us, the kernel is no shorter.

Measured 4297.11 us, ratio 0.9851 (0.982 to 0.9882). The chain:

```profile
1974.53 8.90 DMA h_rows<-ff_acc
...
1989.32 1.77 DMA h_rows<-ff_h_row
```

The two waits are 10.7 us for 15.9, the transposes 25.1 us for 30.3, and the stretch behind them 370.1, for the changed kernel's 369.9: held gathers are not missed. So the four batches held back (the second to the fifth) cost about 5 us in the stores. The rest of these waits, 8.90 us for the first store, was there without them; the first batch's gathers still start beside it, and the cause was not tried. In the time of the kernel 5 us don't show.

### 8. No table switches in the mixer

```diff
-                    act.activation(act_of[:, b % RB], dots[:, b % RB], ACT.Gelu).then_inc(s["gelu"], 1)
+                    act.activation(act_of[:, b % RB], dots[:, b % RB], ACT.Sigmoid).then_inc(s["gelu"], 1)
```

> The changed kernel with a sigmoid in the place of the mixer's 30 gelus, so that no table is loaded between the gates' sigmoids and the batches; this changes tile 0's weights. My step (the loads hide): mixer 525 us unchanged within 3. The rule of the Trainium skill (2.66 us for each switch, 0.3 us of waiting in a unit): 5 to 8 us shorter.

Measured 4292.02 us, ratio 0.9863 (0.981 to 0.9916), the mixer 523.3 us for 527.9. The kernels whose mixer is the changed one's to the letter have 524.8 to 532.2 us there, 529.7 in the mean of eleven. So the switches cost something between 1.5 and 9 us, and the length alone decides neither for "within 3" nor for 5 to 8. Some 2 us of the mean's 6.4 come before the first batch, where this edit changes nothing (198.3 us from the first branch product to the last transpose of tile 0, 200.4 in the mean of the eleven). The waits behind the router say a little more. VectorE's for sigmoids fall from 8.4 to 4.6 us, and TensorE's one wait between gates and outputs from 7.5 to 5.6; beside the gate units of the changed kernel TensorE waited only 0.3 us. ScalarE's timeline of the changed kernel has the load and the gelu behind it, with work ahead of both:

```profile
2510.03 1.12 ACT L2635 ACTIVATE ff_room<-banks 128x512 f32<-128x512 f32 x1
2511.16 1.28 ACT L2542 ACT_TABLE_LOAD   x1
2512.46 0.20 ACT L2542 ACTIVATE ff_gelu<-ff_dots 128x2 f32<-128x2 f32 x1
```

From the end of the copy to the start of gelu it is 1.31 us (2511.15 to 2512.46). Against the Trainium skill ("ScalarE: Activation LUTs", What ACT_TABLE_LOAD costs), which adds a drain of 1.38 us, this trace shows a switch at the load's price alone. So the reason that the rule gives is not seen here, whatever the mixer's length says.

## Why the prediction was right, and where it was not

**Direction and bound: right, the size three quarters.** By medians the change brings 70 us of the 97 and a ratio of 0.985 for 0.978; 4293.5 lies in the band of the sum as made (4215 to 4300), close to its upper edge. A batch beside the mixer that TensorE bounds costs some 0.5 us, and one less ahead of the dense loop gives back about 4 (experiment 5: 72 us from the transposes up to the dense loop for 18).

**The mixer, +97: measured +98.7 by its own first and last instruction, and part of that is luck.** The intervals on the line through [rows 2], the unit of 6.85 us, the 11 us behind the router (9.6) and the gathers hidden in a ring of two came as worked out. One term was not needed: the 10 us for two balanced engines. Beside the gates TensorE was never kept waiting. Two others were too small by about as much: TensorE's work was 478 us for 398 + 73, and the ends with the outputs 40 for 34. So the sum is right within 2 us because errors of 13 and 11 us cancel. The slower case (a landing of 16.7 us) did not come near: the landing stayed at 8.1 us.

**Expert layer to batch 51, -87: measured -74.** Two steps failed. "48 transposes are 22 us and 3 go to a store" was 30.3: the step looked for what the stores in SP's queue stand in front of, and not for what starts beside them, the gathers of five batches (holding four of them gives back 5 us, experiment 7). And "11 half heads of 20.44" took one clean step of before for all of them: the picks of tile 1 in front of `top16` on VectorE make two of them longer, 7 us here, and 1.7 us are the products that take over tile 0's sums. The first and the last of the sixteen would have shown it in the trace of before: its copies (L2197) stand at 2015.20 and 2335.04 us, fifteen steps in 319.8 where 15 x 20.44 is 306.6. The step of 23.87 was right to the hundredth, and experiment 6 takes it away.

**Batch 51 to the dense loop, -107: measured -89.** VectorE's work (385, measured 382.2) and the quads' waits (35.0, now 1.2) were right. The term "the waits for rows I leave at 40" measured 62.6. Of these, 12 us are the beginning of the ring of three, whose places don't follow on those of the ring of five (gone with other places, experiment 4); 9 are gathers that share the DMA engines with a gate block (gone with the write, experiment 2); 42 lie ahead of the dense loop. There the DMA share is 0.95, and 1.01 in experiment 4, so the bytes are the limit for most of it; but only 5 of the 42 us go with the gate block's bytes (experiment 2, share 0.86 over its last 54 us), and the pause in the gathers ahead of it was not tried. The sum went by VectorE's busy time for the whole stretch; its last 50 us don't belong to VectorE. The trace of before would have shown this too (37 us of work in its last 58, at a share of 1.02).

**The second stage: right in its own row and nearly worth nothing.** The sum booked 35 us for it and no price for its place. Experiment 1 has the price: the ring of three costs 37.5 us of waits for rows, for 41.4 us of waits for quads that the second stage saves.

**The rivals.** Too-short rings: true in part. Waits for rows were 23 us over the sum's 40, for 60 more in the rival. Against the ring of five (25.1 us) 12 are the ring's beginning; with that mended 49.6 are left, so some 24 us belong to the length of three or to its meeting the bytes at the end, and the two are not told apart. The mixer's ring was long enough. The table switches: the price of 7 us is not excluded by the mixer's length, but the drain behind it isn't in the trace. That the change brings 97 us as drawn: no, 64 to 70.

## What to carry to other kernels

Move gathers to where TensorE bounds and the DMA engines idle, and price each by what it costs where it leaves: by its bytes where the stretch is short of bytes (5.1 us here), by its dots where VectorE is (2.3). The mean of what stands there is not the price: it holds work that stays. A buffer taken from a ring has the ring's price, and when a ring changes its length, write its places out on both sides of the change: one batch that takes a place two before it cost 12 us of waits. And take a stretch's bound window by window up to its end; the busy share of its whole length hides that the last tenth has another.

## What the runs showed of the hardware

- The interval of a split product follows the columns on a line down to 256: 0.116 to 0.1175 us at 256, 0.157 at 344, 0.177 at 388 (22 of them in 3.90 us, 1746.42 to 1750.32), 0.232 at 512.
- A gathered 1 MB that lands in 7.9 us in the median landed in 16 to 17.5 us beside a 4 MB write, and in 21.4 us beside such a write and the dense loop's first loads. A write cut into four parts left most of the waits where they were (58.9 us for 62.6).
- With VectorE short of work and a DMA share of 1.01, a gathered batch of 2.1 MB costs 4.9 to 5.1 us (experiments 4 and 5).
- The load of another function table takes 1.28 us, and the instructions ahead of it and behind it stand 0.01 to 0.02 us away (2511.15 to 2512.46 us for the load and both gaps).
- The same instructions ahead of the mixer took 1403.5 us in one profile and 1452.8 in another, with TensorE busy for 1173.67 and 1223.30 us and a granted clock of 0.88 and 0.85. No edit is in that stretch; a kernel's time moves by 1.1% through it.
